# A two-block transformer on one Trainium2 core: input x in two token halves, and the order of the first loads

## What is computed

```
mod_x = silu(c) @ w_ada + b_ada          # shift, scale, gate (6 x 1024); mod_c the same from c_ctx
hx = rms_norm(x, norm1_g)   * (1 + sc1)  + sh1
hc = rms_norm(ctx, norm1_g) * (1 + csc1) + csh1
qx, kx, vx, ux = split(hx @ w_in)        # 3 x 512 and 2 x 512 columns
kvc            = hc @ w_in[:, 512:1536]
u = ux[:, :512] * sigmoid(ux[:, 512:])   # then a 31-tap convolution over tokens, layer norm, silu
```

## Time and profile before

| | |
|---|---|
| median of 3 runs | 729.4 us (729.28 to 729.64) |
| the profiled execution | 729.7 us, its span 727.9 us |
| TensorE busy (PE) | 715.3 us, 98% of the span |
| VectorE busy (DVE) | 517.4 us, 71% |
| ScalarE busy (ACT) | 411.2 us, 56% |
| DMA | 145.94 MB, mean 201 GB/s |
| mean granted TensorE clock | 0.999 |

### The profile page before, as it was taken

One profiled execution on the slowest core, in us unless ns is written; L12 is line 12 of the kernel. 1 busy time (PEld: TensorE's weight loads), 2 busy tenths in 40 slices (PEclk: granted clock), 3 DMA queues, 4 the chain that ended last, 5 costly groups with the idle time before them and its releaser, 6 DMA issues.

```text
span 727.9 us, 9700 instructions
## 1 busy us (share of the span) xinstructions
PE 715.3 (98%) x3766; PEld 574.6 (79%) x3766; DVE 517.4 (71%) x911; ACT 411.2 (56%) x691; POOL 24.6 (3%) x43
## 2 busy tenths in 40 slices
PE   7999999999999999999999999999999999999996
PEld 6668885578888888888888777778888888888885
DVE  4689999898666866847898799765857455545544
ACT  4477658986754563556546676675455444344432
POOL 1030012001000000000110000000000000000000
PEclk9999999999999999999999999999999999999999
DMA  9995939617556576643548333453376566555511
GB/s 367 413 378 184 389 105 359 222 59 259 194 186 233 206 280 222 242 174 115 161 167 301 140 117 121 159 178 121 116 231 231 174 185 204 189 174 174 174 58 59
DMA packets 72990, 145.94 MB, mean 201 GB/s; under 512 B 4129, under 2 KB 27681, under 8 KB 71921
## 3 DMA queue, kind: packets, MB, share of 16 engines
q1 hardware_dynamic: 71136, 140.03, 55.0%
q0 software_dynamic: 1520, 5.03, 1.9%
q10 hardware_dynamic: 288, 0.27, 0.1%
HBM read 144.27 MB, written 1.05 MB: 200 GB/s over the span
## 4 chain that ended last, share of the span: by engine, by line
PE 87%; DVE 5%; ACT 2%; DMA 2%; issue 2%; SPq 0%; POOL 0%; POOLq 0%; DVEq 0%
PE bank L441 22%; PE bank L443 22%; PE bank L442 22%; PE bank L785 5%; PE bank L423 5%; PE bank L783 3%; DMA WX<-in_w_ada 2%; DVE WL L1573 2%; PE bank L460 1%; PE bank L917 1%; PE bank L939 1%; PE bank L623 1%; PE bank L782 1%; PE bank L514 1%; PE bank L481 1%
## 5 line engine op out<-in xcount | busy, mean ns | idle before, releaser
L1573 DVE TENSOR_TENSOR WL<-W,WH 128x1024 fp32r<-128x1024 f32 (+2 forms) x222 | 249.6, 1170 | 36.2 <-ACT WH L1070 36.1
L1070 ACT ACTIVATE WH<-W 128x1024 fp32r<-128x1024 f32 (+2 forms) x222 | 211.8, 1011 | 52.2 <-DMA W<-in_w_mlp 36.3
L441 PE MATMUL bank<-WH,AHL 128*128 128x512 f32 (+1 forms) x480 | 189.1, 394 | 0.8 <-DVE WL L1573 0.4
L443 PE MATMUL bank<-WH,AHL 128*128 128x512 f32 (+1 forms) x480 | 185.4, 386 | 0.0
L442 PE MATMUL bank<-WL,AHL 128*128 128x512 f32 (+1 forms) x480 | 185.2, 386 | 0.0
L441 PEld LDWEIGHTS bank<-WH,AHL 128*128 128x128 f32 x480 | 90.2, 188 | 22.8 <-issue 4.0
L443 PEld LDWEIGHTS bank<-WH,AHL 128*128 128x128 f32 x480 | 90.1, 188 | 18.6
L442 PEld LDWEIGHTS bank<-WL,AHL 128*128 128x128 f32 x480 | 90.3, 188 | 16.9
L441 PE MATMUL bank<-WH,HH 128*128 128x512 f32 (+1 forms) x218 | 84.9, 390 | 0.0
L443 PE MATMUL bank<-WH,HL 128*128 128x512 f32 (+1 forms) x218 | 84.5, 388 | 0.0
L442 PE MATMUL bank<-WL,HH 128*128 128x512 f32 (+1 forms) x218 | 84.4, 387 | 0.0
(11 more groups left out here) (287 smaller groups left out, 852.8 us busy)
## 6 DMA issues: line engine op xcount, KB each, us to landing
W<-in_w_mlp SPq DMA_DIRECT2D x32, 1024.0 KB, 5.4
W<-in_w_in SPq DMA_DIRECT2D x24, 1024.0 KB, 5.7
W<-in_w_gate SPq DMA_DIRECT2D x22, 512.0 KB, 4.2
W<-in_w_up SPq DMA_DIRECT2D x22, 512.0 KB, 5.2
W<-in_w_down SPq DMA_DIRECT2D x11, 1024.0 KB, 5.0
W<-in_w_ada SPq DMA_DIRECT2D x10, 1024.0 KB, 8.5
WX<-in_w_ada SPq DMA_DIRECT2D x10, 1024.0 KB, 10.4
W<-in_w_out SPq DMA_DIRECT2D x8, 1024.0 KB, 5.7
```

Of the source, the lines that this page charges most:

```text
L441: e.matmul(po, hs, wh[:, k, c0:c0 + cw], start=first and k == 0, stop=False)
L443: ins = e.matmul(po, ls, wh[:, k, c0:c0 + cw], start=False, stop=last and k == unit.nk - 1)
L1070: e.activation(m.WH[unit.slot][:, c], m.W32[unit.slot][:, c], ACT.Copy).then_inc(S["w_hi"], 1)
L1573: e.tensor_tensor(m.WL[unit.slot][:, c], m.W32[unit.slot][:, c], m.WH[unit.slot][:, c].bitcast(F32), ALU.subtract).then_inc(S["w_lo"], 1)
```

## The change

The diff, cut to its core (`...` marks what is left out):

```
-        self.XT = M("XT", 0, [128, 8, 256])
-        self.xsq = M("xsq", 24, [128, 8, 256])
-        ...
+        self.XT = M("XT", 0, [128, 2, 8, 128])
+        self.xsq = M("xsq", 40, [128, 2, 8, 128])
 # SyncE queue
-    for h in range(2):
-        e.dma_start(m.XT[:, 4 * h:4 * h + 4, :], ...)
-    for n in range(16):
+    x_half(0)
+    load(0)
+    x_half(1)
+    for n in range(1, 15):
         load(n)
     e.dma_start(m.XC[:, :, :], ...)
-    for n in range(16, len(units)):
+    for n in range(15, len(units)):
 # GpSimd
-    w.wait_ge(S["mean_sq"], 2)
-    e.tensor_tensor(m.stat[:, 40:42], m.stat[:, 24:26], ..., ALU.pow).then_inc(S["rstd"], 2)
+    power(0)
+    power(1)
     power(2)
     power(3)
 # TensorE
+    def x_sums(tb):
+        for k in range(8):
+            w.wait_ge(S["sq_sum" if k > 3 else "x_sq"], tb + 1)
+            ins = e.matmul(bank[5 + tb][:, 0:1], m.xsq[:, tb, k, :], m.ones[:, 0:1], start=k == 0, stop=k == 7)
+        ins.then_inc(S["sums"], 1)
+    def x_spread(tb):
+        w.wait_ge(S["rstd"], tb + 1)
+        e.matmul(bank[7][:, tb * 128:tb * 128 + 128], ..., m.ident[:, :], ...).then_inc(S["sums"], 1)
-    keep_busy(11)
+    keep_busy(7)
     x_sums(0)
-    keep_busy(3)
+    keep_busy(2)
+    mod_first(0)
+    x_spread(0)
+    mod_turn(0, 4)
     x_sums(1)
-    mod_first(0)
-    x_spread()
-    mod_turn(0)
-    keep_busy(3)
-    for e8 in range(8):
+    ab(0, 0)
+    x_spread(1)
+    mod_first(1)
+    mod_turn(1, 6)
+    ab(0, 1)
+    for e8 in range(1, 8):
         if e8 < 7:
             mod_first(e8 + 1)
         ab(e8, 0)
 # ScalarE
+    def x_square(tb):
+        w.wait_ge(S[f"l_x{tb}"], 16)
+        for h in range(2):
+            ks = slice(4 * h, 4 * h + 4)
+            e.activation(m.xsq[:, tb, ks, :], m.XT[:, tb, ks, :], ACT.Square, ...)
+    x_square(0)
+    x_square(1)
+    first = high_halves(1)
+    next(first)
+    high_x(0, slice(0, 128))
+    next(first)
+    next(first, None)
+    high_x(0, slice(128, 256))
+    for k in range(1, 7):
         hi()
         high_x(k)
-        if k == 1:
+        if k == 2:
             e.activation(..., ACT.Sigmoid)
-    hi()
     w.wait_ge(S["l_xc"], 16)
     square(2, m.XC[:, 0, :], m.XC2[:, 0, :])
+    hi()
     high_x(7)
+    hi()
     square(3, m.XC[:, 1, :], m.XC2[:, 1, :])
-    hi(2)
+    hi()
 # VectorE
+    x_mean(0)
     rows_out(0)
+    modulation(0)
+    modulate_x0(0)
+    first = low_halves(1)
+    next(first)
+    x_mean(1)
+    next(first)
+    next(first, None)
+    low_x(0, slice(0, 128))
+    modulate_x0(1)
+    e.tensor_copy(m.rB[:, :], bank[7][:, 0:256]).then_inc(S["setup"], 1)
+    low_x(0, slice(128, 256))
+    for k in range(1, 8):
+        rows_out(k)
         modulation(k)
         modulate_x(k)
+        if k == 7:
+            mean_square(2, (2,))
         lo()
         low_x(k)
-    mean_square(2, (2,))
+    hat(m.XC, m.XC2, 0, 2, "c_hat")
+    lo()
     mean_square(3, (3,))
-    lo()
-    hat(m.XC, m.XC2, 0, 2, "c_hat")
     hat(m.XC, m.XC2, 1, 3, "c_hat")
     lo()
```

More of the change, by code:

```diff
@@ L70, in __init__ @@
         self.XC = M("XC", 48, [128, 2, D])
-        self.XT = M("XT", 0, [128, 8, 256])
-        self.xsq = M("xsq", 24, [128, 8, 256])
-        self.xpair = [M(f"xpair{i}", 68 + 2 * i, [128, 2, 256]) for i in range(2)]
-        self.xfour = [M(f"xfour{i}", 73 + i, [128, 256]) for i in range(2)]
+        self.XT = M("XT", 0, [128, 2, 8, 128])
+        self.xsq = M("xsq", 40, [128, 2, 8, 128])
         self.rB = M("rB", 72, [128, 256])
@@ L151 @@
 sq_sum mean_sq rstd ada1_mm rows1_dve rows1_turned mod1_sum mod1
-x_adds l_x mx_dve mx_act kx c_hat c_turned mc_dve mc_act kc
+x_sq l_x mx_dve mx_act kx c_hat c_turned mc_dve mc_act kc
 a_mm b_mm gate_sig u u_turned hp conv_first conv k_mm q_mm v_mm k_out kc_out q_out v_out vc_out rope_mul rotated qk_turned qk_act
@@ L316, in load, with x_half @@
             e.dma_start(v[:, :, c0:c0 + cw], src).then_inc(unit.landing, 16)
-    for h in range(2):
-        e.dma_start(m.XT[:, 4 * h:4 * h + 4, :], d["xt"][h].rearrange("p (k t) -> p k t", k=4)).then_inc(S[f"l_x{h}"], 16)
-    for n in range(16):
+    def x_half(tb):
+        e.dma_start(m.XT[:, tb, :, :], d["xt"][tb].rearrange("p (k t) -> p k t", k=8)).then_inc(S[f"l_x{tb}"], 16)
+    x_half(0)
+    load(0)
+    x_half(1)
+    for n in range(1, 15):
         load(n)
     e.dma_start(m.XC[:, :, :], d["ctx"].rearrange("(t p) n -> p t n", p=128)).then_inc(S["l_xc"], 16)
-    for n in range(16, len(units)):
+    for n in range(15, len(units)):
         if n == 22:
@@ L484, in mod_first, with mod_turn @@
         frees(bk, ("rows1_dve", e8 + 1))
-    def mod_turn(e8):
-        b = turn_bank("rows1_turned")
+    def mod_turn(e8, b=None):
+        b = turn_bank("rows1_turned", b)
         w.wait_ge(S["l_id"], 16)
@@ L502, in x_ready @@
     def x_ready(k):
-        return "kx", k + 1
+        return "kx", k + 2
     def ab(e8, tb):
@@ L510, in ab @@
         ls = m.AL[:, e8, tb * 128:tb * 128 + 128]
-        w.wait_ge(S["mx_act"], e8 + 1)
+        w.wait_ge(S["mx_act"], e8 + 2 if e8 else tb + 1)
         for n in range(2):
@@ L517, in ab @@
             e.matmul(bank[2 * n + tb][:, :], hs, wl[:, 512 * n:512 * n + 512], start=False, stop=False)
-        w.wait_ge(S["kx"], e8 + 1)
+        w.wait_ge(S["kx"], e8 + 2 if e8 else tb + 1)
         for n in range(2):
@@ L521, in ab @@
                      stop=e8 == 7).then_inc(S["b_mm" if n else "a_mm"], 1)
[L523 to L533, removed]
-        w.wait_ge(S["l_id"], 16)
[L535 to L540, removed]
-    keep_busy(11)
+    def x_sums(tb):
[3 more added lines that the diff above has]
+        ins.then_inc(S["sums"], 1)
+        frees(5 + tb, ("mean_sq", tb + 1))
+    def x_spread(tb):
+        w.wait_ge(S["l_id"], 16)
+        w.wait_ge(S["rstd"], tb + 1)
+        e.matmul(bank[7][:, tb * 128:tb * 128 + 128], m.stat[:, 40 + tb:41 + tb].to_broadcast([128, 128]), m.ident[:, :],
+                 start=True, stop=True).then_inc(S["sums"], 1)
+    keep_busy(7)
     x_sums(0)
-    keep_busy(3)
+    keep_busy(2)
+    mod_first(0)
+    x_spread(0)
+    mod_turn(0, 4)
     x_sums(1)
-    mod_first(0)
-    x_spread()
-    mod_turn(0)
-    keep_busy(3)
-    for e8 in range(8):
+    ab(0, 0)
+    x_spread(1)
+    frees(7, ("setup", 5))
+    mod_first(1)
+    mod_turn(1, 6)
+    ab(0, 1)
+    for e8 in range(1, 8):
         if e8 < 7:
@@ L1086, in from_bank, with high_x @@
         copy(o, bank[b][:, cols], done, scale)
-    def high_x(k):
-        w.wait_ge(S["mx_dve"], k + 1)
-        e.activation(m.AH[:, k, :], m.hT[:, k, :], ACT.Identity, bias=m.mod1[:, k, 0, 0:1]).then_inc(S["mx_act"], 1)
+    def high_x(k, ts=slice(0, 256)):
+        w.wait_ge(S["mx_dve"], k + 2 if k else ts.stop // 128)
+        e.activation(m.AH[:, k, ts], m.hT[:, k, ts], ACT.Identity, bias=m.mod1[:, k, 0, 0:1]).then_inc(S["mx_act"], 1)
     def modulate_c(i, n):
@@ L1105, in two @@
         return hT[:, 2 * i:2 * i + 2, :].rearrange("p a b -> p (a b)")
-    def half_of(t, h):
-        return t[:, 4 * h:4 * h + 4, :].rearrange("p a b -> p (a b)")
+    def x_square(tb):
+        w.wait_ge(S[f"l_x{tb}"], 16)
+        for h in range(2):
+            ks = slice(4 * h, 4 * h + 4)
+            e.activation(m.xsq[:, tb, ks, :], m.XT[:, tb, ks, :], ACT.Square,
+                         scale=1.0 / 32).then_inc(S["sq_sum" if h else "x_sq"], 1)
     e.dma_start(m.cs[:, :], d["cs"]).then_inc(S["l_cs"], 16)
@@ L1625, in modulation, with modulate_x0, low_x @@
         fused(m.A1[:, :, k], m.mod1[:, k, 1, :], 1.0, m.n1[:, k:k + 1].to_broadcast([128, 2]), ALU.add, ALU.mult, "mod1")
+    def modulate_x0(tb):
+        ts = slice(128 * tb, 128 * tb + 128)
+        w.wait_ge(S["mod1"], 2)
+        w.wait_ge(S["sums"], (2, 4)[tb])
+        w.wait_ge(S[f"l_x{tb}"], 16)
+        fused(m.hT[:, 0, ts], m.XT[:, tb, 0, :], m.A1[:, 0, 0:1], bank[7][:, ts], ALU.mult, ALU.mult, "mx_dve")
     def modulate_x(k):
         w.wait_ge(S["mod1"], 2 * k + 2)
[L1630 to L1642, removed]
+        w.wait_ge(S["setup"], 5)
+        fused(m.hT[:, k, :].rearrange("p (b t) -> p b t", b=2), m.XT[:, :, k, :], m.A1[:, 0, k:k + 1],
+              m.rB[:, :].rearrange("p (b t) -> p b t", b=2), ALU.mult, ALU.mult, "mx_dve")
+    def low_x(k, ts=slice(0, 256)):
+        w.wait_ge(S["mx_act"], k + 2 if k else ts.stop // 128)
+        fused(m.AL[:, k, ts], m.hT[:, k, ts], m.mod1[:, k, 0, 0:1], m.AH[:, k, ts].bitcast(F32), ALU.add, ALU.subtract, "kx")
     def modulate_c0():
@@ L1663, in vector_program, with x_mean @@
     e.tensor_copy(m.csp[:, :, 0:2], m.cs[:, :].rearrange("p (k r) -> p k r", r=2)).then_inc(S["setup"], 1)
[L1664 to L1671, removed]
-    rows_out(0)
-    for k in range(8):
-        if k:
-            rows_out(k)
+    def x_mean(tb):
+        w.wait_ge(S["sums"], (1, 3)[tb])
+        e.tensor_scalar(col(24 + tb), bank[5 + tb][:, 0:1], EPS, None, ALU.add).then_inc(S["mean_sq"], 1)
+    x_mean(0)
+    rows_out(0)
+    modulation(0)
```

(16 more changed lines are left out.)

2 lines of the change are left out of this document (removed).

## The result

The changed kernel takes 734.03 us (median of 10 runs, 730.49 to 735.62) against 729.38 (10 runs, 729.23 to 730.45): ratio 1.0054, 95% interval 1.0035 to 1.0073, so slower, by 4.7 us. The scatter is new: before, ten runs lie within 1.2 us, now within 5.1. The profiled execution took 735.36 us, span 733.6 (before 729.7 and 727.9).

A forecast was written before the change was run, and what follows sets the result against it. TensorE was taken as the bound, busy 98% of the span. Span 727.9 + 0 (start) + 0.1 (end) = 728.0, with 1.8 around it 729.8, less 0.3 for the median 729.5 us; range 728.8 to 730.8.

The forecast's parts named there:

- the pitch of the sums: First block, TensorE: 16 weight loads of the first sums at a pitch of 0.11 take 1.8 us, ending at 7.2.
- Sum of the start: 0: Start: gains or losses up to 0.61 us vanish in the wait for ada1 3, so net 0.
- rival A: Start, TensorE: its slow level comes later or returns; 730.4 to 732.3 us, middle 731.3, chance 0.13.
- The order of the first block: First block: followed in time, S of half 0 starts at 10.4 and `mod_turn(1)` comes at 15.4 us.
- forecast +0.2 at `mod_turn(1)`: First block: `mod_turn(1)` comes at 15.4 us against 15.18 before, +0.2 us.
- the cover of 0.61: TensorE's wait at 21.76 us for ada1 3, landing at 21.7 regardless; hides start differences up to 0.61 us.
- rival B: Start: about fifteen hand-overs make the chain 1 us longer, less the cover +0.65: 730.1 us, chance 0.20.
- The loads: Start: same bytes reordered; ada1 0 lands near 7.8 instead of 9.04, x half 1 near 9.0 us.
- The end of the stage: ScalarE and VectorE: the 0.79 us wait goes, GpSimd's power delays the second scaling; net +0.1 us.
- The power's wait: End of the stage: GpSimd's power, 0.53 us, with hand-overs 0.08 and 0.15, stands in full on VectorE's path.
- forecast +0.1: End of the stage: second scaling starts at 48.65 us against 48.54 before; net +0.1, bounds 0 and +0.3.
- rival D: End of the stage: the 0.79 us wait goes and the power is hidden, 728.6 us; chance 0.05.

The follow-up runs named there:

- after_wide_sums: The changed kernel with its sixteen sum matmuls taken over 128 columns of ones in place of one: 730.07 us, ratio 1.0006.
- before_7_fillers: The kernel before with the changed kernel's number of fillers, seven, then two, then none: 730.51 us, ratio 1.0015.
- adds_7_fillers: The changed kernel with two VectorE additions per token half, leaving two one-column matmuls per half instead of eight; fillers seven and two: 732.05 us, ratio 1.0031.
- start_alone: The changed kernel with the end of the stage as before, only the start new: 735.13 us, ratio 1.0066.
- after_wide_11: The changed kernel with sums over 128 columns and with eleven and three fillers in place of seven and two: 730.18 us, ratio 1.0015.
- the four profiles named above: Profiles of four kernels with the start and loads of the kernel before; their ada1 3 matmuls start at 21.20, 21.23, 21.48 and 21.20 us.
- tail_alone: The kernel before with only the change's second half, context loaded ahead of ab 7 and new order at the end of the stage: 728.11 us, ratio 0.9982.
- before_pool_late: The kernel before with one more wait on GpSimd, holding its later transfers and fills until the context is scaled: 728.33 us, ratio 0.9984.
- after_11_fillers: The changed kernel with eleven fillers before the first sums and three behind them, in place of seven and two: 731.03 us, ratio 1.0032.

## Why the prediction was wrong, point by point

**The step that failed** is the pitch of the sums: "8 matmuls, 16 weight loads at a pitch of (0.52 - 0.19)/3 = 0.11: 1.8 us, to 7.2". The pitch is of four loads at 6.89 us, behind 22 passes of fillers. The changed kernel has 14 passes before its sums, whose first weight load starts at 5.70; the earlier trace rows had the fillers at 421 ns at 5.1 us. So it was readable that the sums might begin at the slow level. Measured: 3.41 us for a forecast 1.8, and twice, since the second sums were slow too. With it falls the term "Sum of the start: 0": `mod_first(3)` came 6.6 us late. Behind them the level stayed slow, mainly by the one column of the sums (`after_wide_sums`: 3.8 us back). Fewer fillers cost too (`before_7_fillers`: 1.0 us in the old order), and so can TensorE's wait for the second half (`adds_7_fillers`).

**The rival A named the mechanism** and got its chance wrong (0.13) and its size too small: up to 2.7 us in the start, measured 6.6 (28.31 against 21.76), with the cost of the order in it. Half of its 2.8 + 2.1 would be 2.45; how it comes to 2.7 isn't said. It took half of the slow work to be hidden in waits; but on this chain nearly every slow matmul is what somebody waits for, and both sums stand on it. The argument against A, that "through those old waits the fillers stayed at 275 ns", compared waits and not what TensorE did between them; what no row of the kernel before could show, a level that falls again, three later profiles show. The Trainium skill ("TensorE: Matmul & The Clock Gate", "Part 1: The HAM clock gate") has activity release the gated clock; the runs agree, and show beyond it that sums of one column did not do what the same sums over 128 columns did.

**The order of the first block.** The hand-overs between S of half 0 and `mod_turn(1)` were right: 5.0 us forecast (10.4 to 15.4), 5.0 measured at the fast level. Its beginning was not: S at 10.4 needs fast sums at 5.4 us. Behind seven fillers the first sums were slow in the profiles of the changed kernel and of `after_wide_sums` and fast in that of `start_alone`, where S comes at 10.84; behind eleven, in `after_wide_11`, it comes at 12.19. So with eleven fillers the forecast +0.2 at `mod_turn(1)` is +2.0, the cover of 0.61 is used up, and the start costs 1.35 us or more at the fast level, the size that rival B put at 0.65; B's cause, many hand-overs each a little longer, isn't what the rows show, since the 5.0 us held. Even in `start_alone`, where the first sums happened to be fast (first turn at 9.76), the level fell again and the second turn came at 17.13; 5.0 us after S would have been 15.84. The cover itself was read from one execution: that ada1 3 "lands at 21.7 whatever came before" does not hold, since in the four profiles named above it was in by 21.2 to 21.5.

**The loads** were right: ada1 0 was in before TensorE asked for it, x half 1 was squared at 8.74 (forecast 9.0).

**The end of the stage** was right in its order and wrong in one duration. The power's wait is 0.66 us with its hand-overs, where 0.76 was forecast. But the scaling was taken as 1.2 us from a trace in which GpSimd issued transfers and filled tiles beside both. Without that two take 1.41 us in place of 2.35: 0.94 of the 1.1 to 1.3 us gained. The forecast +0.1 is -1.3 in `tail_alone`. Its 728.11 lies near rival D's 728.6, but not by D's mechanism: the power was not hidden, and `before_pool_late` has nearly the gain with the 0.80 us wait still there.

Sum at the medians, each against its own kernel before: end -1.3, start's order +1.35, level +3.8 (`after_wide_sums`), together +3.9 of the 4.7 measured. With the order at 1.6 to 1.9, as against the four other profiles, it is 4.1 to 4.4. The rest stays open. `after_wide_11`, fast from its sums on in the profile, should by -1.3 and +1.6 to +1.9 stand 0.3 to 0.6 above the kernel before; its profiled span is 0.2 above, its median 0.9.

The scatter of 5 us fits a level that is reached, and lost again, at different times in different runs. The five runs of the changed kernel with a mean granted clock of 0.999 took 734.7 to 735.6 us, the five with 0.996 to 0.998 took 730.5 to 733.3. The profile of a run of the first kind (735.36 us) has long durations up to 21.7 us and no window below 1.00 there; that of `start_alone` (731.0 us, 0.995) has fast first sums and one fall to 0.50. What in a run decides between them was not tried.

## What to carry to other kernels

A duration is good only for the state it was read in: before moving work to an earlier time, look at what the same instruction took there, and on VectorE look at what GpSimd did beside it. Fillers that look like idle turns are work: count what a change leaves of them ahead of TensorE's first long chain, keep it from idling while it waits in that chain, and make helper matmuls wide where width is free. Take the halves of a bundled change apart first: here 728.11 us was hidden under 734.

## What the runs showed of the hardware

TensorE's first slow stretch, from the first filler on, does not show in the granted clock of the windows (1.00 from 3 to 20 us in the changed kernel); it shows in weight loads of 333 ns for 190, in 128-column passes of 421 ns for 275, and in sixteen small matmuls that take 1.94 us for 1.07. A later fall does show: 0.50 at 13 to 15 us in `start_alone` and `adds_7_fillers` and at 19 to 22 us in `after_11_fillers`, with the long durations again (two passes of 512 columns in 1.05 us for 0.63). So 0.50, the level of 1.2 GHz, goes with the long durations and 1.00, that of 2.4 GHz, with the short ones, and a 1.00 ahead of the first rise says nothing.

VectorE's scaling of 1024 columns in SBUF with one tensor input takes 0.75 us with GpSimd idle, 1.2 us beside later issues and fills, 0.94 with a fill beside its first 0.4 us, and 0.75 beside the issue of the rotation tables. It works the other way too: that issue took 0.95 us beside a scaling and 0.59 otherwise, and tiny fills 0.64 beside one and 0.17 otherwise. The Trainium skill ("SBUF — State Buffer", "SBUF: two separate sides") has the two engines share a pair of ports, taken as an exclusive lock for a whole instruction, where VectorE runs in a two-port mode; the trace agrees that they hinder each other, while 0.75 becoming an even 1.2 is not told apart here from a start that is held back.
